# Experts' first two weights as the stationary operand, in 128 x 128 blocks, with the 96 routed rows streaming past them

## The reference, cut to what matters

```python
def expert(args):
    w1e, w3e, w2e, ie, ge = args
    xe = jnp.take(xt, ie, axis=0)                       # 96 rows of 1024
    hid = jax.nn.silu(xe @ w1e) * (xe @ w3e)            # 96 x 2816
    return (hid @ w2e).astype(jnp.float32) * ge[:, None]
```

## Time and profile before

| | us |
|---|---|
| median of 2 runs | 2115.1 (2113.89 to 2116.31) |
| the profiled execution | 2114.79 |
| its span, first to last instruction | 2113.0 |
| PE busy / DVE busy / ACT busy / POOL busy | 2021.7 / 1609.9 / 1337.5 / 76.4 |

### The profile page before, as it was taken

How to read it: one execution, slowest core, us unless ns; L and a number is a source line. 1 busy time by engine, 2 the same in 40 slices (tenths; PEclk the granted TensorE clock), 3 DMA queues, 4 the chain that set the end, 5 groups by cost and what they waited for, 6 DMA issues and landing times.

```text
span 2113.0 us, 27664 instructions
## 1 busy us (share of the span) xinstructions
PE 2021.7 (96%) x10732; PEld 1548.7 (73%) x10732; DVE 1609.9 (76%) x1135; ACT 1337.5 (63%) x1017; POOL 76.4 (4%) x38
## 2 busy tenths in 40 slices
PE   6999997969679999999999999999999999999998
PEld 5899996758557777777777777777767777777775
DVE  4247764673468888888888888888888888888886
ACT  4234432661357777777777777777777777777774
POOL 0000000000200000000000000000000000000000
PEclk9999998979889999999999999999999999999999
DMA  5222223035469999999999999999999999999994
GB/s 154 73 68 78 89 75 141 3 126 196 161 226 380 373 372 389 364 389 360 387 368 383 375 364 395 358 397 365 386 372 375 386 360 396 357 390 367 383 381 147
DMA packets 190066, 618.27 MB, mean 293 GB/s; under 512 B 12224, under 2 KB 35776, under 8 KB 190016
## 3 DMA queue, kind: packets, MB, share of 16 engines
q1 hardware_dynamic: 186432, 604.99, 76.3%
q0 software_dynamic: 3584, 12.58, 2.6%
HBM read 597.09 MB, written 20.45 MB: 292 GB/s over the span
## 4 chain that ended last, share of the span: by engine, by line
PE 93%; DVE 3%; DMA 2%; ACT 1%; issue 0%; SPq 0%; POOL 0%; ACTq 0%; POOLq 0%; DVEq 0%
PE pair L517 28%; PE pair L519 28%; PE pair L518 28%; PE pair L578 2%; PE pair L811 1%; DMA q_t<-queries_and_keys 1%; PE pair L651 1%; PE pair L740 1%; PE pair L673 1%; PE pair L763 1%; PE pair L636 0%; DMA hg<-projected 0%; DMA x_in<-x 0%; PE pair L618 0%; PE pair L662 0%
## 5 line engine op out<-in xcount | busy, mean ns | idle before, releaser
L1506 DVE TENSOR_TENSOR chunk_low<-ring,chunk_high 128x2048 fp32r<-128x2048 f32 (+1 forms) x382 | 1175.5, 3087 | 225.1 <-ACT chunk_high L1050 225.1
L1050 ACT ACTIVATE chunk_high<-ring 128x3072 fp32r<-128x3072 f32 (+1 forms) x384 | 979.4, 2559 | 213.7 <-PE pair L519 213.4
L517 PE MATMUL pair<-chunk_high,xe_high 128*96 128x512 f32 (+1 forms) x1536 | 579.5, 377 | 1.3 <-DVE xe_low L1500 1.3
L519 PE MATMUL pair<-chunk_high,xe_low 128*96 128x512 f32 (+1 forms) x1536 | 575.3, 375 | 0.0
L518 PE MATMUL pair<-chunk_low,xe_high 128*96 128x512 f32 (+1 forms) x1536 | 573.1, 373 | 0.0
L517 PEld LDWEIGHTS pair<-chunk_high,xe_high 128*96 128x96 f32 x1536 | 248.2, 162 | 90.0 <-DVE chunk_low L1506 2.5
L519 PEld LDWEIGHTS pair<-chunk_high,xe_low 128*96 128x96 f32 x1536 | 247.7, 161 | 90.3
L518 PEld LDWEIGHTS pair<-chunk_low,xe_high 128*96 128x96 f32 x1536 | 248.6, 162 | 87.4
L517 PE MATMUL pair<-chunk_high,hid_high 128*96 128x512 f32 x704 | 280.2, 398 | 0.0
L519 PE MATMUL pair<-chunk_high,hid_low 128*96 128x512 f32 x704 | 277.1, 394 | 0.0
L518 PE MATMUL pair<-chunk_low,hid_high 128*96 128x512 f32 x704 | 275.8, 392 | 0.0
(11 more groups left out here) (202 smaller groups left out, 1828.7 us busy)
## 6 DMA issues: line engine op xcount, KB each, us to landing
ring<-w SPq DMA_DIRECT2D x288, 1536.0 KB, 9.3
ring<-w SPq DMA_DIRECT2D x96, 1024.0 KB, 8.3
raw_w<-w_in SPq DMA_DIRECT2D x16, 1024.0 KB, 5.6
projected<-stage SPq DMA_DIRECT2D x36, 128.0 KB, 1.7
wo_raw<-w_out SPq DMA_DIRECT2D x8, 512.0 KB, 3.2
x_in<-x SPq DMA_DIRECT2D x6, 512.0 KB, 8.2
queries_and_keys<-qk_raw SPq DMA_DIRECT2D x8, 384.0 KB, 2.7
x_again<-x SPq DMA_DIRECT2D x6, 512.0 KB, 5.0
```

Of the source, the lines that this page charges most:

```text
L517: pe.matmul(dst, a_high, b_high, start=first, stop=False)
L519: return pe.matmul(dst, a_low, b_high, start=False, stop=last)
L1050: act.activation(ch[c % SPLIT][:, 0:n], ring[c % RING][:, 0:n], ACT.Copy).then_inc(ch_done, 1)
L1506: dve.tensor_tensor(cl[c % SPLIT][:, 0:n], ring[c % RING][:, 0:n], ch[c % SPLIT][:, 0:n].bitcast(F32), ALU.subtract).then_inc(cl_done, 1)
```

## The change

The two operands of the first two products change places. A 128 x 128 block of a weight chunk (high or low part) is now stationary, and a k-tile of the rows (96 columns) is moving. The result is 128 hidden columns by 96 rows, already transposed as the third product wants it. For each of an expert's 22 column tiles, 8 k-tiles and 2 weights there are three matmuls of 96 columns: high block x high rows, high block x low rows, low block x high rows, all into the tile's own 96 columns of an accumulator that takes four tiles to a PSUM bank. PSUM is now two tensors of 2048 columns; `quad[0]` holds w1's tiles, `quad[1]` w3's, and the last bank of each holds half of the third product. The row transposes use the banks of `quad[0]`.

The transposes of `hid` are gone (PE), with the reads that followed them. In their place ACT writes silu of w1's tiles to `gate_activation` in two operations a block, DVE multiplies in two, ACT makes the high part of the block from `hid` in SBUF in one operation and DVE the low part in one. Five of the 24 chunk low parts (chunks 5, 8, 11, 17 and 21, all of 2048 columns) move from DVE to POOL; PE and SP wait for them on `pool_low`. POOL scatters an expert's result in the next expert's turn, after the gather, and frees `y_rows` after its first low part. The third product and all transfers keep their sizes.

```diff
+LOW_BY_POOL = [5, 8, 11, 17, 21]
+SILU = {LAST[b, 0] + 1: b for b in range(NB)}
+HID = {LAST[b, 1] + 1: b for b in range(NB)}
+HID_HIGH = {LAST[b, 1] + 2: b for b in range(NB)}
+HID_LOW = {LAST[b, 1] + 3: b for b in range(NB)}
+XE_AT = {len(UP) + 4: 0, len(UP) + 5: 1}
...
+    def accumulator(m, i, n=1):
+
+        at = (i // 4) * 512 + (i % 4) * SLOTS
+        return quad[m][:, at:at + n * SLOTS]
...
+    def wait_low(eng, e, c):
+
+        if c in LOW_BY_POOL:
+            eng.wait_ge(pool_low, e * POOL_LOWS + (LOW_BY_POOL.index(c) + 1))
+        else:
+            eng.wait_ge(cl_done, e * DVE_LOWS + (c + 1 - sum(1 for p in LOW_BY_POOL if p < c)))
...
         def expert(e, last):
             for c in range(CHUNKS):
-                pe.wait_ge(cl_done, e * CHUNKS + (c + 1))
+                wait_low(pe, e, c)
...
-                    if c == FIRST[b, 0]:
-                        pe.wait_ge(silu_done, e * NB + (b + 1))
-                    if c == FIRST[b, 1]:
-                        pe.wait_ge(hid_done, e * NB + (b + 1))
-                    for k in range(n):
-                        for c0 in range(0, BLOCK_W[b], 512):
-                            cols = slice(c0, min(c0 + 512, BLOCK_W[b]))
-                            mm = split_mm((PA, PB)[m][0:SLOTS, cols], xeh[:, k0 + k, :], xel[:, k0 + k, :],
-                                          hi[:, k, cols], lo[:, k, cols], k0 + k == 0, k0 + k == KT - 1)
+                        pe.wait_ge(xel_done, e * 2 + 2)
+                    if c == FIRST[b, m]:
+                        pe.wait_ge((silu_done, hid_done)[m], e * NB + (b + 1))
+                    for i in range(BLOCK_TILES[b]):
+                        for k in range(k0, k0 + n):
+                            mm = split_mm(accumulator(m, i), hi[:, k - k0, tile(i)], lo[:, k - k0, tile(i)],
+                                          xe_split[:, k, 0, :], xe_split[:, k, 1, :],
+                                          k == 0 and i % 4 == 0, k == KT - 1 and i in (3, BLOCK_TILES[b] - 1))
...
-                    for i in range(n):
-                        mm = pe.transpose(TB[g][:, i * SLOTS:(i + 1) * SLOTS], hid[:, tile(k0 + i)],
-                                          ident[0:SLOTS, 0:SLOTS])
-                    mm.then_inc(t_mm, 1)
...
+                if c in SILU:
+                    b = SILU[c]
+                    n = BLOCK_TILES[b]
+                    act.wait_ge(used, e * CHUNKS + (LAST[b, 0] + 1 + SPLIT))
+                    act.wait_ge(hid_done, e * NB + (b + 1))
+                    for at in range(0, n, 4):
+                        w = min(4, n - at)
+                        ins = act.activation(gate_act[:, at:at + w, :],
+                                             accumulator(0, at, w).rearrange("p (t s) -> p t s", t=w), ACT.Silu)
+                    ins.then_inc(silu_done, 1)
+                if c in HID_HIGH:
+                    b = HID_HIGH[c]
+                    t0, n = BLOCK_TILE_AT[b], BLOCK_TILES[b]
+                    act.wait_ge(hid_done, e * NB + (b + 2))
+                    act.activation(hid_h[:, t0:t0 + n, :], hid[:, 0:n, :], ACT.Copy).then_inc(hidh_done, 1)
...
             for cc in range(2, CHUNKS + 2):
-                if cc < CHUNKS or not last:
+                if (cc < CHUNKS or not last) and cc % CHUNKS not in LOW_BY_POOL:
                     chunk_low(e, cc)
...
+            if e >= 1:
+                scatter(e - 1)
+            for c in LOW_BY_POOL:
+                chunk_low(e, c)
+                if e >= 1 and c == LOW_BY_POOL[0]:
+                    pool.wait_ge(y_out, 16 * e)
+                    pool.sem_inc(y_free, 1)
```

More of the change, by code:

```diff
@@ L92 @@
 CHUNK = 3 * D
[L93 to L96, removed]
+BLOCK_TILES = [w // P for w in BLOCK_W]
+BLOCK_TILE_AT = [a // P for a in BLOCK_AT]
+LOW_BY_POOL = [5, 8, 11, 17, 21]
+POOL_LOWS = len(LOW_BY_POOL)
+DVE_LOWS = CHUNKS - POOL_LOWS
+SILU = {LAST[b, 0] + 1: b for b in range(NB)}
[3 more added lines that the diff above has]
+XE_AT = {len(UP) + 4: 0, len(UP) + 5: 1}
 def build(nc, x, norm1, w_in, lbf, lbb, hgw, qw, kw, lams, subw, w_out, norm2, rw, w1, w3, w2,
@@ L227, in build @@
     cl = [sb(moe, f"chunk_low{i}", [P, CHUNK], F32R) for i in range(SPLIT)]
-    pair = [perm.enter_context(nc.psum_tensor(f"pair{i}", [P, 1024], F32)) for i in range(4)]
+    quad = [perm.enter_context(nc.psum_tensor(f"quad{i}", [P, 2048], F32)) for i in range(2)]
+    pair = [quad[i // 2][:, (i % 2) * 1024:(i % 2 + 1) * 1024] for i in range(4)]
     PA, PB, PC, PD = pair
@@ L1510, in expert @@
             for cc in range(2, CHUNKS + 2):
-                if cc < CHUNKS or not last:
+                if (cc < CHUNKS or not last) and cc % CHUNKS not in LOW_BY_POOL:
                     chunk_low(e, cc)
                 c = cc - 2
-                if c < len(UP) and c == LAST[UP[c][0], 1]:
-                    b = UP[c][0]
-                    own = hid[:, BLOCK_AT[b]:BLOCK_AT[b] + BLOCK_W[b]]
+                if c in HID:
+                    b = HID[c]
+                    n = BLOCK_TILES[b]
+                    dve.wait_ge(used, e * CHUNKS + (LAST[b, 1] + 1 + SPLIT))
@@ L1517, in expert @@
                     dve.wait_ge(silu_done, e * NB + (b + 2))
[L1518 to L1525 removed]
+                    dve.wait_ge(hidl_done, e * NB + (b + 1))
@@ new lines, in expert @@
+                    for at in range(0, n, 4):
+                        w = min(4, n - at)
+                        ins = dve.tensor_tensor(hid[:, at:at + w, :], accumulator(1, at, w).rearrange("p (t s) -> p t s", t=w),
+                                                gate_act[:, at:at + w, :], ALU.mult)
+                    ins.then_inc(hid_done, 1)
+                if c in HID_LOW:
+                    b = HID_LOW[c]
+                    t0, n = BLOCK_TILE_AT[b], BLOCK_TILES[b]
+                    dve.wait_ge(hidh_done, e * NB + (b + 1))
+                    dve.tensor_tensor(hid_l[:, t0:t0 + n, :], hid[:, 0:n, :], hid_h[:, t0:t0 + n, :].bitcast(F32),
+                                      ALU.subtract).then_inc(hidl_done, 1)
@@ L1554, in _, with scatter @@
         gather(0)
-        for e in range(EXPERTS):
-            if e + 1 < EXPERTS:
-                pool.wait_ge(t_mm, e * T_PER_EXPERT + 2)
-                gather(e + 1)
+        def scatter(e):
             pool.wait_ge(y_ev, e + 2)
+            if e >= 1:
+                pool.wait_ge(y_out, 16 * e)
             pool.indirect_dma_start(out=out, out_offset=bass.IndirectOffsetOnAxis(ap=token[:, e:e + 1], axis=0),
@@ L1562, in _, with chunk_low @@
                                     compute_op=ALU.add).then_inc(y_out, 16)
-            pool.wait_ge(y_out, 16 * (e + 1))
-            pool.sem_inc(y_free, 1)
+        def chunk_low(e, c):
+            n = chunk_size(c)
+            pool.wait_ge(ch_done, e * CHUNKS + c + 1)
+            pool.tensor_tensor(cl[c % SPLIT][:, 0:n], ring[c % RING][:, 0:n], ch[c % SPLIT][:, 0:n].bitcast(F32),
+                               ALU.subtract).then_inc(pool_low, 1)
+        for e in range(EXPERTS):
+            if e + 1 < EXPERTS:
+                pool.wait_ge(t_mm, 2 * e + 2)
+                gather(e + 1)
+            if e >= 1:
+                scatter(e - 1)
+            for c in LOW_BY_POOL:
+                chunk_low(e, c)
+                if e >= 1 and c == LOW_BY_POOL[0]:
+                    pool.wait_ge(y_out, 16 * e)
+                    pool.sem_inc(y_free, 1)
+        scatter(EXPERTS - 1)
+        pool.wait_ge(y_out, 16 * EXPERTS)
     moe.close()
```

84 lines of the change are left out of this document (32 added, 52 removed).

## The result

The changed kernel takes 4770.8 us (4770.44 to 4771.15, 2 runs) against 2115.1 us: 2.26 times the time of before, 95% interval 2.250 to 2.261. The forecast was 3000 us. The sign and the bound were right, the size was not, and 4770.8 us lies 21 us above the stated range, whose top was set by the rival "the clock falls during the up-products" at 4700 us. That rival is what happened.

The account below looks back on a forecast made before the run. PE was taken to bound the kernel at 94.1 us an expert. Less 63.0 removed, plus 118.3 for 1056 loads, gave 149.4; 55.3 more times 16 is +885 us, so 3000 us, range 2900 to 4750.

Parts of the forecast that it names:

- the clock falls during the up-products: Rival, PE in the up-products: clock at its 1.2 GHz level, 0.2125 us a matmul, +2582, 4700 us; chance 0.25.
- What bounds the kernel now: Whole expert before the change: PE sets the pace at 94.1 us, with the transfers close behind.
- The sum of starts: PE in one expert before: matmul and transpose counts times their start spacings give 94.2 us against 94.1 measured.
- 1056 loads, each as dear as its columns, at the full clock: PE in an expert's up-products after the change: 128-column loads bound it, 0.112 us each, 118.3 us; chance 0.55.
- PE never goes idle, a load is always running: PE in the up-products: argument that the clock would stay at 1.00, against the half-clock case of 4700 us.
- The price of the half clock: PE in the up-products at half clock: 0.2125 us a load with its matmul, 224.4 us an expert; chance 0.25.
- What else moves ... I count nothing: ACT, DVE, POOL, transfers and PE's waits: all have more cover as the period grows by 55 us; nothing added.
- POOL's cover: POOL's five low parts, 4.4 us each, finish before PE needs them; tightest chunk 21, 1.0 us spare; failure at most 352 us.
- The other rivals: PE's up-products: short matmuls as dear as float32, 0.223 us, 4875 us, chance 0.08; or loads hidden, 1972 us, chance 0.09.
- The forecast that gains: PE's up-products: loads run ahead, 0.051 us a matmul, 1972 us; gain from 0.060 us downward; chance 0.09.

Follow-up runs that it names:

- experiment 11: The kernel before with only the five low parts on POOL and the scatter in the next expert's turn: 2142.7 us against 2114.8, ratio 1.013.

## Why the prediction was wrong, point by point

- **What bounds the kernel now** was right. The sum of starts, 94.2 against 94.1 us, is the model with which every experiment was then forecast. One slip beside it changes nothing: 34.6 MB in 94.1 us are 368 GB/s; the 377 is what the window measured.
- **1056 loads, each as dear as its columns, at the full clock**: right, by 0.11 us in the written-out change before its clock falls, 0.11 with 192 columns (117.9 us an expert against the 118.3 of the sum), and by the halving to 0.06 with half the load. The total of 3000 us at the full clock is met by the written-out version with 192 columns, 2995.2 us. The change itself never ran so.
- **The step that failed** is "PE never goes idle, a load is always running" as the reason against the clock's fall, with which I gave that rival 0.25 and the full clock 0.55. Unbroken loads did not keep the clock up. With PE never idle, the written-out change fell to clock 0.50 and 0.213 us a matmul in each of the last 15 experts (the first began there), where I had counted 1.00 and 0.112. Under the same loads, the runs with 96 columns lost the clock, those with 128 held it but did not raise it, and those with 192 raised it. What I had against the rival was an absence ("no stretch of this trace with unbroken loads is at half clock"). But that trace has no float32r matmul below 256 columns, so it held no long stretch of short streams under unbroken loads that could have spoken either way. The row for the rival, the fall at 447 us with PE working in bursts, did not settle it either, since PE was idle between the bursts there; the evidence did not carry 0.55 against 0.25.
- **The price of the half clock** was nearly right: 0.2125 us from L618, 0.213 measured, and 224.4 us of up-products an expert, forecast and measured. (That the two are equal to the tenth has some luck in it: 225.3 us at half clock, less those first moments at the full clock.) For that case 4700 us were forecast and 4770.8 measured. The 71 us between them are 42.2 us of idle time at the jumps and 1.8 x 16 = 28 us of the third product, which starts at half clock in every expert; neither is in the rival's sum. The range ended at 4750, with only 50 us above the rival that it had to hold; it left no room for a new wait.
- **"What else moves ... I count nothing"**: wrong by the idle times. The new wait was not among the semaphores, where I looked, but at the loop's jump: the body grew 2.7 times and the jump began to cost 2.1 to 4.3 us. What PE waits for there stays open.
- **POOL's cover** held: no wait of PE in the change is put down to POOL. The version with the low parts back on DVE is 17 us faster, but 6 of these lie in shorter idle times at the jumps and 11 in up-products that began with a little more time at the full clock. POOL's low part of 2048 columns took 4.5 us when nothing was beside it, 4.4 forecast. In the faster kernel before, the same move costs 28 us. I had missed that DVE and POOL can block each other (below).
- **The other rivals** did not occur: a short matmul costs 0.06 us when its load is short, and no version hid a load of 128 columns below 0.11 us.
- **The forecast that gains** had its condition at 0.060 us a matmul; the version with half-length loads came to it (64.4 us an expert, 0.061 a matmul), and only by leaving half of the work out. Two loads in place of three still give 2443 us. None of the runs points to a version of this exchange that beats the kernel before: 352 blocks x 2 loads x 0.112 = 79 us stand against the 63 that they replace.

## What to carry to other kernels

On PE count the loads beside the streams: an exchange of operands that streams a quarter fewer columns but makes the streams shorter than the loads turns the loads into the bound. Then ask what the array's own activity will be: a stretch that is full of loads and thin in columns can lose the clock, and its matmuls and loads then take nearly twice the time (0.213 us a pair against 0.112); here useless columns under the same loads made the kernel 1.56 times faster (4770.8 to 3058.3 us). And where a loop's body grows a few times, look for an idle time at its jump back, with a count equal to the number of jumps; unrolling was worth 63 us with wide streams, 100 us in the change itself, and 1559 us where the gap cost the clock as well.

## What the runs showed of the hardware that I had not expected

**The clock has a memory.** With 128 streamed columns the same up-products ran at 1.00 when they were entered without a gap, and at 0.50 for some 225 us when a gap of 2 to 4 us came first (4660.1 and 3101.0 us). With 192 columns the clock fell after 12 of the 14 gaps, and each time it was back within 7 us while the streams ran on.

**A jump back can cost 2 to 4 us of PE.** It came at all 14 jumps in each looped version of the change, also in those of two loads, whose body has 844 matmuls. It never came in the kernel before, whose body has 450, and never in the written-out ones, although these too fetch 2.2 to 2.9 MB of instructions.

**DVE and POOL block each other.** In the changed kernel the low part of `hid` for the third block and POOL's low part (start us, duration us):

```profile
1099.29 5.19 DVE L1543 TENSOR_TENSOR hid_low<-hid,hid_high 128x576 fp32r<-128x576 f32 x1
...
1098.86 5.00 POOL L1588 TENSOR_TENSOR chunk_low<-ring,chunk_high 128x2048 fp32r<-128x2048 f32 x1 [24.37 <-ACT chunk_high L1063]
```

And the same operation of DVE with the low parts back on DVE:

```profile
1097.36 0.75 DVE L1543 TENSOR_TENSOR hid_low<-hid,hid_high 128x576 fp32r<-128x576 f32 x1
```

5.19 against 0.75 us: DVE ended only when POOL had (1103.86). The Trainium skill says it in "SBUF — State Buffer", in the section "Who interferes with whom": VectorE and GpSimd share a pair of ports under an exclusive lock, and a VectorE instruction with two inputs in SBUF contends with a GpSimd instruction that reads SBUF. The trace agrees, and by that rule the moved low parts should have been priced before the run. It holds the other way round too, and it spares an operation that reads one input from PSUM; both are in experiment 11:

```profile
1047.79 0.95 DVE L1529 TENSOR_TENSOR hid<-pair,hid 96x768 f32<-96x768 f32 x1 [1.29 <-PE pair L529]
...
1046.00 4.65 POOL L1577 TENSOR_TENSOR chunk_low<-ring,chunk_high 128x2048 fp32r<-128x2048 f32 x1 [19.18 <-ACT chunk_high L1060]
...
1097.51 8.36 DVE L1516 TENSOR_TENSOR chunk_low<-ring,chunk_high 128x3072 fp32r<-128x3072 f32 x2 [3.57 <-ACT chunk_high L1060]
...
1104.48 5.89 POOL L1577 TENSOR_TENSOR chunk_low<-ring,chunk_high 128x2048 fp32r<-128x2048 f32 x1 [5.10 <-ACT chunk_high L1060]
```

DVE's `hid`, with one input in PSUM, took 0.95 us in the middle of POOL's operation, its time without POOL. POOL's low part that began while DVE's two low parts ran (to 1105.87) took 5.89 us in place of 4.65. So the change itself exposed `hid_low`: before, it read PSUM; after, it reads SBUF only.
